# Two PSUM bank pairs exchanged and three weight splits moved in an odd attention layer (Trainium2, one core)

## The reference

```python
xm = rms_norm(h, g_pre) * (1 + sc_m) + sh_m        # stream 0, 256 x 1024
cm = rms_norm(hc, g_pre) * (1 + csc_m) + csh_m     # stream 1, the context
q, k, v = split(xm @ w_qkv)                        # 16 query heads, 4 key heads of 64
q, k = rms_norm(q per head) * q_g, rms_norm(k per head) * k_g
_, kc, vc = split(cm @ w_qkv)                      # kc normed as k
q, k = apply_rope(q), apply_rope(k)
y = softmax(q @ [k, kc].T * 64**-0.5) @ [v, vc]
h = h + gt_m * rms_norm(y @ w_out_c, g_post)
```

## Time and profile before

| | |
|---|---|
| runs | 2005.47, 2005.93, 2006.95 us (median 2005.93) |
| the profiled execution | 2004.89 us, its span 2003.1 us |
| mean granted TensorE clock | 0.988 |
| busy: PE | 1927.0 us (96%) |
| busy: DVE | 1281.9 us (64%) |
| busy: ACT | 912.7 us (46%) |
| DMA, mean over the span | 160 GB/s |

### The profile page before, as it was taken

How to read it: one execution, slowest core, us unless ns; L and a number is a source line. 1 busy time by engine, 2 the same in 40 slices (tenths; PEclk the granted TensorE clock), 3 DMA queues, 4 the chain that set the end, 5 groups by cost and what they waited for, 6 DMA issues and landing times.

```text
span 2003.1 us, 28769 instructions
## 1 busy us (share of the span) xinstructions
PE 1927.0 (96%) x11994; PEld 1638.1 (82%) x11994; DVE 1281.9 (64%) x1700; ACT 912.7 (46%) x1266; POOL 14.1 (1%) x17
## 2 busy tenths in 40 slices
PE   6999989999999999899999989999999989989998
PEld 5788968888888888788879868988888879679997
DVE  4775796766576669776664563765554366757775
ACT  5344545334533454543464254543333254655553
POOL 0000000000000000000000110000000000000000
PEclk9999999999999999899999999999999999999999
DMA  6676425766476642776452310222222322114552
GB/s 270 251 274 228 173 104 205 256 255 235 163 266 255 234 170 95 265 271 241 144 185 86 126 64 22 103 87 101 89 88 101 105 85 85 43 64 142 192 190 88
DMA packets 45489, 320.62 MB, mean 160 GB/s; under 512 B 5041, under 2 KB 5169, under 8 KB 6961
## 3 DMA queue, kind: packets, MB, share of 16 engines
q1 hardware_dynamic: 38592, 270.09, 37.1%
q10 hardware_dynamic: 6768, 48.69, 6.3%
HBM read 317.72 MB, written 1.05 MB: 159 GB/s over the span
## 4 chain that ended last, share of the span: by engine, by line
PE 89%; DVE 6%; ACT 2%; issue 1%; DMA 1%; POOLq 0%; POOL 0%; SPq 0%; DVEq 0%; ACTq 0%
PE ps L523 87%; DVE s_wl L1857 2%; PE ps L860 1%; DVE s_big L2136 1%; ACT s_wh L1215 1%; PE ps L723 0%; DMA s_ca<-in_c_all 0%; PE ps L700 0%; DVE s_tmp L1945 0%; DMA s_big<-in_bias 0%; DVE s_tmp L2365 0%; DVE s_xx L1857 0%; DVE s_X L2055 0%; PE ps L822 0%; ACT s_tmp L1485 0%
## 5 line engine op out<-in xcount | busy, mean ns | idle before, releaser
L523 PE MATMUL ps<-s_xx,s_wh 128*128 128x512 f32 (+1 forms) x3328 | 903.2, 349 | 17.8 <-DVE s_wl L1857 15.8
L1857 DVE TENSOR_TENSOR s_wl<-s_raw,s_wh 128x2048 fp32r<-128x2048 f32 x215 | 493.1, 2295 | 308.7 <-ACT s_wh L1215 308.6
L523 PE MATMUL ps<-s_xx,s_wl 128*128 128x256 f32 (+1 forms) x2208 | 672.7, 305 | 6.9 <-DVE s_wl L1857 6.5
L523 PEld LDWEIGHTS ps<-s_xx,s_wh 128*128 128x128 f32 x3328 | 582.8, 191 | 113.0 <-DVE s_wl L1857 20.3
L1215 ACT ACTIVATE s_wh<-s_raw 128x2048 fp32r<-128x2048 f32 x215 | 408.8, 1907 | 147.8 <-PE ps L523 147.3
L523 PEld LDWEIGHTS ps<-s_xx,s_wl 128*128 128x128 f32 x2208 | 421.4, 191 | 26.7 <-DVE s_wl L1857 6.9
L523 PE MATMUL ps<-s_wh,s_hl 128*128 128x512 f32 (+1 forms) x608 | 232.7, 383 | 2.4 <-DVE s_hl L1938 2.3
L523 PE MATMUL ps<-s_wh,s_hh 128*128 128x512 f32 (+1 forms) x608 | 230.2, 379 | 0.0
L523 PE MATMUL ps<-s_wl,s_hh 128*128 128x512 f32 (+1 forms) x608 | 230.1, 379 | 0.0
L523 PE MATMUL ps<-s_wh,s_xx 128*128 128x256 f32 x928 | 179.4, 287 | 0.0
L523 PEld LDWEIGHTS ps<-s_wh,s_xx 128*128 128x128 f32 x928 | 148.2, 191 | 5.0 <-issue 4.1
(11 more groups left out here) (232 smaller groups left out, 1673.8 us busy)
## 6 DMA issues: line engine op xcount, KB each, us to landing
s_big<-in_w_ada ACTq DMA_DIRECT2D x46, 1024.0 KB, 5.9
s_raw<-in_ffn_gate SPq DMA_DIRECT2D x44, 1024.0 KB, 5.5
s_raw<-in_ffn_up SPq DMA_DIRECT2D x44, 1024.0 KB, 4.8
s_raw<-in_ffn_down SPq DMA_DIRECT2D x44, 1024.0 KB, 4.8
s_raw<-in_w_up SPq DMA_DIRECT2D x44, 1024.0 KB, 4.8
s_raw<-in_w_down SPq DMA_DIRECT2D x22, 1024.0 KB, 4.8
s_raw<-in_w_in SPq DMA_DIRECT2D x18, 1024.0 KB, 4.8
s_raw<-in_w_in_ab SPq DMA_DIRECT2D x10, 1024.0 KB, 4.8
```

The lines of the kernel that those rows point to most:

```text
L523: return pe.matmul(o, lhsT, rhs, start=start, stop=stop, skip_group_check=True)
L1857: dve.tensor_tensor(wide(wl, u), raw[:, u % SLOTS, :].rearrange("p (k n) -> p k n", k=8), f32(wide(wh, u)), SUB).then_inc(*w_low.tick(u))
```

## The change

In `turn_bank` and `odd()`, banks 0 and 1 change roles with 4 and 5: units 0 and 1 of w_qkv go to banks 0 and 1, which held the transposes of stream 0; the transposes of pieces 0 and 1 of stream 1 go to banks 4 and 5, and with them later users. The transposes of pieces 0 and 1 of stream 1 move from step 12 of unit 1 to step 0 of unit 4, those of pieces 2 and 3 from step 0 to step 6. On ScalarE and VectorE the split of w_qkv unit 4 moves behind the first evictions of stream 1 (on ScalarE behind `bound_root(P[1], 0)`, on VectorE behind `bound_resid(P[1])`), that of unit 5 behind the k copies (ScalarE) and the root of q1 (VectorE), and that of w_out_c unit 2 from n = 6 of the attention to behind its loop. No instruction is added or removed.

```diff
-                     ("f", 0, 0): (0, 1, 2, 3), ("f", 0, 1): (0, 1, 2, 3), ("m", 1, 0): (4, 5, 6, 7)}
+                     ("f", 0, 0): (0, 1, 2, 3), ("f", 0, 1): (4, 5, 2, 3), ("m", 1, 0): (4, 5, 6, 7)}
@@ tensor, odd()
-                chunks(u[0], [4], [("odd", "q", 0)], 256, xw[0], True, 0)
-                freed[4] = copied["odd", "q", 0]
-                chunks(u[1], [5], [("odd", "q", 1)], 256, None, True, 0, {12: lambda: bound_turn(P[1], 0, 1)})
-                freed[5] = copied["odd", "q", 1]
+                chunks(u[0], [0], [("odd", "q", 0)], 256, xw[0], True, 0)
+                freed[0] = copied["odd", "q", 0]
+                chunks(u[1], [1], [("odd", "q", 1)], 256, None, True, 0)
+                freed[1] = copied["odd", "q", 1]
                 chunks(u[4], [6, 7], [("odd", "k main", c) for c in range(2)], 256, None, True, 0,
-                       {0: lambda: bound_turn(P[1], 2, 3)}, at=(0, True), last=False)
+                       {0: lambda: bound_turn(P[1], 0, 1), 6: lambda: bound_turn(P[1], 2, 3)}, at=(0, True), last=False)
...
                 def step1():
-                    scale("k0", 0, 1)
+                    scale("k0", 0, 5)
...
-                    scale("q2", 4, 4)
-                    root("q3", 0, 5, 0)
+                    scale("q2", 4, 0)
+                    root("q3", 0, 1, 0)
...
-                    scale("q3", 0, 4)
+                    scale("q3", 0, 0)
...
-                chunks(u[2], [0], [("odd", "q", 2)], 256, aside={3: step0, 11: step1})
-                freed[0] = copied["odd", "q", 2]
-                chunks(u[3], [1], [("odd", "q", 3)], 256, aside={3: step2})
-                freed[1] = copied["odd", "q", 3]
+                chunks(u[2], [4], [("odd", "q", 2)], 256, aside={3: step0, 11: step1})
+                freed[4] = copied["odd", "q", 2]
+                chunks(u[3], [5], [("odd", "q", 3)], 256, aside={3: step2})
+                freed[5] = copied["odd", "q", 3]
@@ scalar, odd()
                 bound_high(P[0], pre_mixer(1), 0, 1, 2, 3)
-                high_after(unit["w_down", 10])
                 for b in range(4):
                     bound_squares(P[1], b, 4 + b, P[0])
                 bound_root(P[1], 0)
+                high_after(unit["w_down", 10])
                 stream_squares(P[1])
                 bound_root(P[1], 1)
                 high_after(u[0])
                 high_after(u[1])
                 bound_high(P[1], pre_mixer(1), 0, 1, 2, 3)
-                high_after(u[4])
...
                 copy("k0", 0, 6, "k_g", ("odd", "k raw", 0))
                 copy("k1", 1, 7, "k_g", ("odd", "k raw", 1))
+                high_after(u[4])
                 root("q0", 2, 0)
...
                 for n in range(2, len(H.units) + 3):
                     attend(H, n)
-                    if n == 6:
-                        high_after(u[5])
+                high_after(u[5])
@@ vector, odd()
                 bound_low(P[0], pre_mixer(1), 0, 1, 2, 3)
-                low_after(unit["w_down", 10])
                 for b in range(3):
                     bound_evict(P[1], b, 4 + b)
                 bound_sum(P[1], 0)
                 bound_evict(P[1], 3, 7)
                 bound_resid(P[1])
+                low_after(unit["w_down", 10])
                 bound_norm(P[1])
                 low_after(u[0])
                 low_after(u[1])
                 bound_low(P[1], pre_mixer(1), 0, 1, 2, 3)
-                low_after(u[4])
...
                 root("q0", 2, 2)
                 root("q1", 3, 0)
+                low_after(u[4])
                 turn_k(0)
...
                 for n in range(2, len(H.units) + 3):
                     attend(H, n)
-                    if n == 6:
-                        low_after(u[5])
+                low_after(u[5])
```

More of the change, by code:

```diff
@@ L1741, in root @@
                     act.wait_ge(*product["odd", "root", {"k0": "k1", "q0": "q1"}.get(x, x)])
-                    act.activation(hcol[:, 16 * n:16 * n + 8], ps[{"q3": 5}.get(x, 2)][:, at:at + 8], ACT.Sqrt,
+                    act.activation(hcol[:, 16 * n:16 * n + 8], ps[{"q3": 1}.get(x, 2)][:, at:at + 8], ACT.Sqrt,
                                    bias=v("eps6")).then_inc(*rooted.tick(("odd", x)))
@@ L1752, in odd @@
                 root("k1", 1, 8)
-                square("q0", 2, 4, ("odd", "q", 0))
-                square("q1", 3, 5, ("odd", "q", 1))
+                square("q0", 2, 0, ("odd", "q", 0))
+                square("q1", 3, 1, ("odd", "q", 1))
                 copy("k0", 0, 6, "k_g", ("odd", "k raw", 0))
                 copy("k1", 1, 7, "k_g", ("odd", "k raw", 1))
+                high_after(u[4])
                 root("q0", 2, 0)
                 root("q1", 0, 8)
-                square("q2", 4, 0, ("odd", "q", 2))
+                square("q2", 4, 4, ("odd", "q", 2))
                 high_after(u[2])
@@ L1763, in odd @@
                     act.activation(Ko[:, n, 256:512], T(n)[:, 256:512], ACT.Copy).then_inc(*copied.tick(("odd", "k ctx", n)))
-                copy("q0", 2, 4, "q_g", ("odd", "q", 0))
-                copy("q1", 3, 5, "q_g", ("odd", "q", 1))
+                copy("q0", 2, 0, "q_g", ("odd", "q", 0))
+                copy("q1", 3, 1, "q_g", ("odd", "q", 1))
                 root("q2", 1, 0)
@@ L1771, in odd @@
                                    ACT.Copy).then_inc(*copied.tick(("odd", "k", kv)))
-                square("q3", 0, 1, ("odd", "q", 3))
+                square("q3", 0, 5, ("odd", "q", 3))
                 high_after(u[3])
-                copy("q2", 4, 0, "q_g", ("odd", "q", 2))
+                copy("q2", 4, 4, "q_g", ("odd", "q", 2))
                 root("q3", 2, 0)
-                copy("q3", 0, 1, "q_g", ("odd", "q", 3))
+                copy("q3", 0, 5, "q_g", ("odd", "q", 3))
                 attend(H, 0)
@@ L2576, in odd @@
                 root("k1", 1, 1)
-                scale("k0", 0, 1, ("odd", "k raw", 0))
+                scale("k0", 0, 5, ("odd", "k raw", 0))
                 scale("k1", 1, 3, ("odd", "k raw", 1))
@@ L2593, in odd @@
                 turn_q(1, 3, 7)
-                scale("q2", 4, 4, ("odd", "q", 2))
+                scale("q2", 4, 0, ("odd", "q", 2))
                 root("q3", 0, 2)
@@ L2597, in odd @@
                 turn_q(2, 4, 6)
-                scale("q3", 0, 4, ("odd", "q", 3))
+                scale("q3", 0, 0, ("odd", "q", 3))
                 turn_q(3, 0, 7)
```

## The result

| | before | after |
|---|---|---|
| median of four runs | 2005.7 us (2005.42 to 2006.95) | 1988.8 us (1988.04 to 1990.53) |
| ratio | | 0.9916, 95% interval 0.9900 to 0.9931 |
| the profiled execution | 2004.89, span 2003.1 | 1989.06, span 1987.3 |
| mean granted clock | 0.988 | 0.989 |

The forecast was 1990.0 us (1987 to 1996). The profiled executions differ by 15.83 us, where 15.9 were forecast. That agreement is partly luck: the changed code gained 0.8 us more than forecast, and 0.9 us was lost where nothing was changed, as the last column of this table shows. Its times are those of TensorE, counted from the start of the last down projection matmul, so that what happened earlier in the program is left out.

A forecast was written before the change was run, and what follows sets the result against it. TensorE, holding 89% of the span, was taken as the bound, with three gaps and the lowered clock behind them. Gains of 6.9 + 1.6 + 2.4 (10.9) and 5.05, together 15.9 us off 2005.93, gave 1990.0 us, range 1987 to 1996.

The forecast's parts named there:

- The gap was for the bank, not for the split that the profile named: TensorE's 6.54 us gap ending at 1643.26: unit 0 waits for PSUM bank 4's eviction, which stands behind unit 4's split.
- the change doesn't do what it says: Rival: the gap at 1643.26 was for something else and remains; 1996.9 us, chance 0.04.
- Units 0 and 1 run at once, norm 0.87 earlier, new gap 1.4 us: Units 0 and 1 run without wait from 1636.6 to 1648.1; norm at 1648.5 instead of 1649.37; TensorE then waits 1.4 us.
- the wait only changes its name: Rival: units 0 and 1 start early but stream 1's chain on VectorE and ScalarE is no earlier; near 1992, chance 0.08.
- hidden on both engines: Unit 4's moved split was claimed covered on ScalarE and VectorE; without VectorE's cover it would cost the norm up to 1.9 us.
- x_low's last piece as the second bound: Stream 1 half of unit 4: last low piece ready at 1661.2, as TensorE reaches it; 6.9 us gained up to the roots.
- The roots and the clock: 1.6 + 2.4: Root matmuls after the k projection start without the 1.47 us gap, 1.6 us; clock stays up for eight following steps, 2.4.
- The split of unit 5 on VectorE, 0.1: In the q part, the moved 2.29 us split delays k's rope 0.65; idle time absorbs all but 0.1 us.
- The rival was wrong for this change: Rival: VectorE becomes the q part's bound, unit 5's split not absorbed; 2.2 to 5.6 us lost, 1992 to 1996, chance 0.1.
- The attention, 5.05: Taking w_out_c unit 2's split out of the attention saves 5.05 us, clock included; behind the loop it costs nothing.
- The clock at the new gap: At the new 1.4 us gap ahead of stream 1's transposes, near 1649, the clock was expected to stay at 1.00.
- The chance of 0.17: Rival: the clock falls at the new gap for 6.8 us, costing 3.4 us; 1993.3 us, chance 0.17.

The follow-up runs named there:

- the three kernels of the last group: Changed kernel with stream 1 transposes at steps 4 and 8 of unit 4 (1990.53 us), unit 3's split behind stream 1's low pieces (1988.98), or both (1987.2).
- the doubled split: Changed kernel with VectorE making the low part of w_qkv unit 5 twice in its new place: 1990.86 us, ratio 0.9931.

## Why the prediction was right, and where it was off

The stage in every combination that was run:

| stage, us | banks as before | banks exchanged |
|---|---|---|
| no split moved | 70.04 | 62.50 |
| split of unit 4 moved | 67.29 | 61.60 |
| split of unit 5 moved | 65.26 | 60.84 |
| both moved | not run | 58.37 |

The parts alone would add to 7.54 + 2.75 + 4.78 = 15.07; together they give 11.67. The banks and the split of unit 4 work on the same standstill: with the banks exchanged TensorE has two units of work until the norm, and the earlier evictions then shorten a gap by the 0.9 by which the norm comes sooner. Moved last, with unit 5's already moved, the split of unit 4 brings 2.47, because the shorter gap also leaves the clock up.

How much each part brings alone is less sure than that each brings something. All cells but the last (58.37) have stays at the low clock in them, and how long one lasts can differ by trace. By medians beside the kernel before, the banks alone bring 5.8 us, the split of unit 4 alone 2.3 and that of unit 5 alone 3.1. The banks come first, unit 5 second and unit 4 third by either measure.

- **The gap was for the bank, not for the split that the profile named.** Right, and shown by the move of that split alone: the gap shrank by 2.20 while the split itself ran after it. The rival that the change doesn't do what it says is out.
- **Units 0 and 1 run at once, norm 0.87 earlier, new gap 1.4 us.** Right: 0.88 and 1.29, and the rival that the wait only changes its name is out by that. But the moved split is not "hidden on both engines", as I wrote beside a sum that counted it. The evictions start 2.19 us earlier and the norm only 0.88; from the residual to the norm takes 5.57 us (1643.83 to 1649.40) where it took 4.25 (1645.12 to 1649.37). ScalarE's split is covered, that of VectorE is a link of the chain (above) and costs the norm 1.3 us, about the length of the new gap. No run puts it elsewhere; unit 4 is the next that TensorE multiplies by, so there is little room to put it later.
- **x_low's last piece as the second bound.** Forecast 1661.2; it started at 1661.34, of which 0.91 is the later start, so by its length of 0.69 it ended at about 1661.1 on the forecast's scale. That gap and pieces bind side by side is what the three kernels of the last group show: 0.06, nothing, and 1.42 together.
- **The roots and the clock: 1.6 + 2.4. The mechanism was right, the size too small**, and this is the step that was off. The move of unit 5's split alone brought 4.78 against these 4.0. I costed the 16 two-column matmuls at their old 2.47 us at the new place too; at full clock they occupy 1.71 (1664.80 to 1666.51) against 2.33 before (1672.39 to 1674.72), 0.6 less. The scales behind them occupy 3.49 (1669.46 to 1672.95), another 0.2 less than before. The clock had fallen within the roots, and was not quite back in the scales; I had counted the eight steps between them alone. The price of the clock itself is that of one trace of the kernel before, 6.8 us low; other traces with this gap have 3.4 or none.
- **The split of unit 5 on VectorE, 0.1.** The path was as forecast: split at 1675.28 (forecast 1675.15), rope of k at 1677.48 (1677.35), idle time of 0.53 used up. Of the 0.1 nothing is seen at the last rope. That this is the edge, not the middle, of the cover is shown by the doubled split: 2.28 us more work, 2.33 us more time. The rival was wrong for this change, but only just.
- **The attention, 5.05** (14.40 - 9.33 is 5.07). Measured 5.08. That the freed split costs nothing behind it is seen in the unchanged 232 us to the end.
- **The clock at the new gap.** It stayed at 1.00, as forecast, but the reason I gave is not borne out. I had held the two-column matmuls behind the 1.47 us gap against it; with the banks exchanged alone, the same gap with the same matmuls left the clock at 1.00. What stands is the rows themselves: gaps of 1.29 and 1.30 at the new place left it up in all six traces that have one, as did the 1.40 before. None of these has two-column matmuls right behind it, so they can't say whether those matter. The chance of 0.17 was for something that was one moved split away (2.17 us, clock down).

The sum: forecast 15.95 for stage and attention, measured 16.75; the 0.8 more are the roots and scales. The 0.91 lost before the stage hid this in the total.

## What to carry to other kernels

When the profile names a long operation as what a gap waited for, ask what the waiting instruction really reads or writes; here it was a PSUM bank whose eviction stood behind that operation in the same queue, and moving the bank alone was worth 5.8 us by medians where moving the operation was worth 2.3. Two waits that end close to each other hide each other's cure: a fix that gains nothing alone may be half of one that does (0.06, nothing, and 1.42 together). Measure such edits between two fixed instructions of the trace rather than over the whole run, and look there whether the clock fell, since that alone moves such a length by more than a microsecond. Put a split or a copy where its engine idles, not where its operand happens to be ready.

## What the runs showed of the hardware that was not expected

**The same gap does not always cost the same.** Gaps of TensorE in this stage and the attention, over the traces of this case; the stay at 0.50 behind the gap is worked out from windows as above. At the last two gaps, and at some of those of 3.46 and 3.47, the clock had fallen within the gap already.

| gap, us | where | clock after it |
|---|---|---|
| 1.29 or 1.30, ahead of the transposes | changed kernel, both traces, and four of its variants | 1.00 |
| 1.47, before the roots | before | 0.50 for some 6.8 us |
| the same | unit 5's split back; unit 4's split moved alone | 0.50 for some 3.4 us |
| the same | banks alone | 1.00 throughout |
| 2.17 | unit 4's split back; banks alone | 0.50 for some 3.4 us |
| 3.46 or 3.47, in the attention | before; unit 4's split moved alone; banks alone | 0.50 for some 3.4 us |
| the same | attention's split back; unit 5's split moved alone | 0.50 for over 6 us |
| 4.34 | unit 4's split moved alone | 0.50 for some 5.4 us |
| 6.54 | before | 0.50 for some 3.0 us |

The instructions around the 1.47 us gap are the same in all four kernels; what differs is, among other things, the time since the earlier standstills, and when in the run the gap falls. What decides isn't settled here: no run varied the one with the other fixed. The attention shows the same: one gap, and the stretch took 64.75 to 64.81 us in three traces and 66.03 and 66.14 in two. For a forecast it means that one and the same gap of 1.47 us cost between nothing and 3.4 us beyond its length (half of 6.8).

**Untouched stages differ between traces by more than a microsecond.** In one stage that neither the change nor an experiment touches, with many standstills, the granted clock was 0.81 before and 0.87 after over the same 27 us:

```profile
290.00:317.00 27.00, 20.93 (x169) 14.90 (x168) 22.14 (x55) 15.53 (x32) 0.00 (x0) 0.81 0.59 216
```

```profile
290.00:317.00 27.00, 21.52 (x177) 15.54 (x178) 22.52 (x53) 15.07 (x30) 0.00 (x0) 0.87 0.62 223
```

The next projection of the chain started at 318.43 before and 317.11 after, 1.3 us earlier; by the last down matmul the changed kernel was 0.91 us later. Over all traces that matmul started between 1635.71 and 1638.70. The 0.91 of the first section is within this spread, and a difference of one microsecond between single profiled executions as wholes says nothing.
